# Idle matmuls on TensorE in every eighth expert, another order in the PLE stage, and the last gate tile computed in two parts

## The reference

```
for i in range(2):
    x = x + mixer_i(rmsnorm(x) * norm_mix[i])      # 0: dilated attention, 1: latent attention (MLA)
    x = x + moe(rmsnorm(x) * norm_moe[i])          # 32 experts, top 1 group of 4, top 2 experts in it
    gate = sigmoid((rmsnorm(x) * norm_ple[i]) @ ple_w_gate[i])     # (256,1024) @ (1024,1024)
    x = x + (p[i] @ ple_w[i]) * gate
return rmsnorm(x) * norm_final
```

## Time and profile before

| what | value |
|---|---|
| median of 3 runs | 1388.43 us (1388.11, 1388.43, 1392.02) |
| the profiled execution | 1391.07 us, its span 1389.2 us |
| PE busy | 1057.8 us, 76% of the span |
| DVE, ACT busy | 457.7 us, 292.8 us |
| DMA | 469.97 MB, 338 GB/s over the span |
| mean granted clock of PE | 0.901 |

### The profile page before, as it was taken

One profiled execution on the slowest core, in us unless ns is written; L12 is line 12 of the kernel. 1 busy time (PEld: TensorE's weight loads), 2 busy tenths in 40 slices (PEclk: granted clock), 3 DMA queues, 4 the chain that ended last, 5 costly groups with the idle time before them and its releaser, 6 DMA issues.

```text
span 1389.2 us, 30964 instructions
## 1 busy us (share of the span) xinstructions
PE 1057.8 (76%) x13756; PEld 821.9 (59%) x13756; DVE 457.7 (33%) x1017; ACT 292.8 (21%) x555; POOL 9.2 (1%) x19
## 2 busy tenths in 40 slices
PE   6999999988666667667667989976666666666667
PEld 6999999865545445444445645555444444444446
DVE  6545555552212111111114666521121211121127
ACT  5433444220100000000004444310000000000016
POOL 1000000000000000000000000000000000000000
PEclk9999999999988877988898999998888888898899
DMA  9996540699999999999999740499999999999980
GB/s 272 310 239 175 159 119 0 267 367 426 425 426 426 427 426 426 426 426 426 426 427 393 276 177 1 148 425 427 426 426 426 427 426 426 426 426 427 426 365 35
DMA packets 113483, 469.97 MB, mean 338 GB/s; under 512 B 4656, under 2 KB 78512, under 8 KB 88528
## 3 DMA queue, kind: packets, MB, share of 16 engines
q1 hardware_dynamic: 112672, 465.78, 83.7%
q0 software_dynamic: 688, 2.28, 0.4%
HBM read 467.00 MB, written 1.05 MB: 337 GB/s over the span
## 4 chain that ended last, share of the span: by engine, by line
DMA 49%; PE 44%; DVE 3%; issue 2%; ACT 1%; DVEq 0%; SPq 0%; ACTq 0%
DMA ring<-moe_w_down 33%; DMA ring<-moe_w_up 8%; PE ps L1608 6%; DMA ring<-ple_w_gate 5%; PE ps L1379 5%; PE ps L1380 5%; PE ps L1381 5%; PE ps L1623 4%; PE ps L1695 3%; DMA ring<-moe_w_gate 3%; PE ps L1493 2%; PE ps L1653 2%; PE ps L1514 1%; PE ps L1443 1%; PE ps L1419 1%
## 5 line engine op out<-in xcount | busy, mean ns | idle before, releaser
L1608 PE MATMUL ps<-ring,scr 128*32 128x128 f32 x8192 | 291.2, 302 | 161.3 <-DMA ring<-moe_w_up 103.8
L1608 PEld LDWEIGHTS ps<-ring,scr 128*32 128x32 f32 x8192 | 252.6, 122 | 202.2 <-DMA ring<-moe_w_up 115.0
L1623 PE MATMUL ps<-ring,scr 128*32 128x256 f32 x2048 | 170.0, 485 | 114.8 <-DMA ring<-moe_w_down 100.6
L1623 PEld LDWEIGHTS ps<-ring,scr 128*32 128x32 f32 x2048 | 83.5, 134 | 183.3 <-issue 103.7
L1131 DVE TENSOR_TENSOR scr<-scr,ps 128x128 f32<-128x128 f32 x64 | 23.8, 372 | 445.9 <-PE ps L1608 445.9
L716 ACT COPY scr<-ps 32x256 f32<-32x256 f32 x128 | 46.8, 366 | 557.2 <-PE ps L1623 556.5
L1144 DVE COPY scr<-ps 32x256 f32<-32x256 f32 x128 | 53.3, 416 | 239.0 <-PE ps L1623 238.2
L1379 PE MATMUL ps<-hT_hi,w_qk_hi 128*128 128x256 f32 x368 | 104.4, 284 | 0.0
L1381 PE MATMUL ps<-hT_hi,w_qk_lo 128*128 128x256 f32 x368 | 103.7, 282 | 0.0
L1380 PE MATMUL ps<-hT_lo,w_qk_hi 128*128 128x256 f32 x368 | 103.6, 281 | 0.0
L1653 PE MATMUL ps<-scr 128*128 128x512 f32 x128 | 63.1, 639 | 15.5 <-DVE scr L1144 15.5
(11 more groups left out here) (239 smaller groups left out, 1182.3 us busy)
## 6 DMA issues: line engine op xcount, KB each, us to landing
ring<-moe_w_gate SPq DMA_DIRECT2D x64, 2048.0 KB, 36.0
ring<-moe_w_up SPq DMA_DIRECT2D x64, 2048.0 KB, 36.4
ring<-moe_w_down SPq DMA_DIRECT2D x64, 2048.0 KB, 36.3
ring<-dsa_w_in SPq DMA_DIRECT2D x72, 512.0 KB, 6.8
ring<-ple_w_gate SPq DMA_DIRECT2D x4, 2048.0 KB, 37.3
ring<-dsa_w_out SPq DMA_DIRECT2D x2, 2048.0 KB, 13.6
ring<-mla_w_out SPq DMA_DIRECT2D x2, 2048.0 KB, 24.5
x_sb<-ple_w SPq DMA_DIRECT2D x2, 1024.0 KB, 6.2
```

The lines of the kernel that those rows point to most:

```text
L1608: mm = pe.matmul(bank(b)[CW * q:CW * q + CW, 0:P], xT[:, k, :], tile(t + j, KD, FF)[:, k, P * q:P * q + P], start=(k == 0), stop=(k == KD ...
L1623: mm = pe.matmul(bank(6)[CW * q:CW * q + CW, 0:T], e_hT[:, CW * j:CW * j + CW], tile(t + 2, FF // P, D)[:, j, T * q:T * q + T], start=(j = ...
```

## The change

Three things are changed together.

1. **Idle matmuls.** In the eighth expert of each pass PE runs two matmuls of `ident` by 512 columns of `hs` into bank 6 after the `gate` matmuls and two after the `up` matmuls (`stay_busy`). Nobody reads them.
2. **The start of the PLE stage.** `EARLY` is 2. ACT copies chunk 0 of x first, makes 2 high pieces, copies chunk 1, casts the turned x and then makes the other 6. DVE splits nothing before its copies. PE no longer waits for all 8 high pieces: it takes each k as it comes, and runs low by high two steps behind high by high.
3. **The tail.** The last (chunk 1, half 1) is computed in two parts of `PART` = 256 columns, in banks 3 and 2 (`gate_part`); in layer 0 the turn of chunk 0 stands between the parts. ACT takes the squares of both first halves, and DVE that of chunk 1's second half. Sigmoid, product and sum of the last tile run in two parts. In the final norm DVE multiplies the first half by the gain (`final_gain`) and ACT by the reciprocal (`final`), DVE does the second half, and SP stores four pieces of 256 KB.

The core of the diff:

```diff
-EARLY = 5
+EARLY = 2
+GATES = 5
+PART = 256
 ACT, ple(l):
-                act.wait_ge(S("scattered"), (NGRP + 1) * l + NGRP)
+                take_x(0)
                 high_gate(0, range(EARLY))
-                take_x(0)
-                high_gate(0, range(EARLY, KD))
                 take_x(1)
...
+                high_gate(0, range(EARLY, KD))
                 high_gate(1, range(KD))
...
+                i = 3 * l + 3
+                for c in range(TC):
+                    wait_x(act, i, c, 0)
+                    act.activation(junk_pd[c], x_sb[:, c, 0:512], ACT.Square, accum_out=ss[:, c, 0:1]).then_inc(S("sq_d"), 1)
                 table(ACT.Sqrt)
...
+                table(ACT.Sigmoid)
+                for h in range(2):
+                    act.wait_ge(S("pg_ready"), GATES * l + 4 + h)
+                    act.activation(p_sig[:, 1, 512 + PART * h:512 + PART * h + PART], bank(3 - h)[:, 0:PART], ACT.Sigmoid,
+                                   scale=rstd[:, 1:2]).then_inc(S("sig_ready"), 1)
                 table(ACT.Sqrt)
-                norm_chunk(3 * l + 3, 1)
+                if l == 1:
+                    final(0)
...
 DVE, ple(l):
-                low_gate(0, range(EARLY - 1))
                 for c in range(TC):
                     take_x(c)
...
-                low_gate(0, range(EARLY - 1, KD))
+                low_gate(0, range(KD))
...
                 for c in range(TC):
                     add(c, 0)
-                    square(i, c)
-                for c in range(TC):
-                    add(c, 1)
-                    roots(i, c, c + 1)
-                    finish(c)
+                add(0, 1)
+                if l == 1:
+                    final_gain(0)
+                roots(i, 0, 1)
+                finish(0)
+                if l == 1:
+                    final_gain(1)
+                link(add_part(l, 0))
+                add_part(l, 1).then_inc(S("x_added"), 1)
+                wait_x(dve, i, 1, 1)
+                last = x_sb[:, 1, 512:D]
+                dve.tensor_tensor_reduce(out=junk_pa[1], in0=last, in1=last, scale=1.0, scalar=0.0,
+                                         op0=ALU.mult, op1=ALU.add, accum_out=ss[:, 1, 1:2]).then_inc(S("sq_a"), 1)
+                roots(i, 1, 2)
+                finish(1)
...
 PE, experts(l):
+                def stay_busy():
+                    for _ in range(2):
+                        pe.matmul(bank(6), ident, hs[:, 0, 0:4, :], start=True, stop=True)
...
                             mm.then_inc(S("gate_ready" if j == 0 else "up_ready"), 1)
+                            if i == BODY - 1:
+                                stay_busy()
...
 PE, ple(l):
+                def gate_part(h):
+                    if h == 1:
+                        pe.wait_ge(S("sig_ready"), GATES * l + 2)
+                    cols = slice(PART * h, PART * h + PART)
+                    for x_k, w in ((hT_hi, g_hi), (hT_lo, g_hi), (hT_hi, g_lo[l])):
+                        for k in range(KD):
...
+                for k in range(EARLY, KD):
+                    for c in range(TC):
+                        high_by_high(c, k)
+                    low_by_high(k - EARLY)
...
+                gate_part(0)
+                if l == 0:
+                    turn_rows(3, 0)
+                gate_part(1)
```

More of the change, by code:

```diff
@@ L122, in used @@
             return ("gate_ready", "up_ready", "down_ready")[n % 3], NE * l + n // 3 + 1
-        return "pg_ready", 2 * TC * l + TC * (t - Tiles.PLE[l] + 1)
+        return "pg_ready", GATES * l + (GATES if t > Tiles.PLE[l] else TC)
 C_ID, C_LOW, C_CAUSAL = 0, 128, 256
@@ L731, in experts, with final @@
                     act.wait_ge(S(f"o_down{l}"), NE + 1)
+            def final(c):
+                act.wait_ge(S("x_gained"), c + 1)
+                act.wait_ge(S("rstd_ready"), 6 * TC + c + 1)
+                act.activation(x_sb[:, c, 0:512], p_w[:, c, 0:512], ACT.Copy, scale=rstd[:, c:c + 1]
+                               ).then_inc(S("final_a"), 1)
             def ple(l):
@@ L770, in ple @@
                     sigmoid(c, n)
+                i = 3 * l + 3
+                for c in range(TC):
+                    wait_x(act, i, c, 0)
+                    act.activation(junk_pd[c], x_sb[:, c, 0:512], ACT.Square, accum_out=ss[:, c, 0:1]).then_inc(S("sq_d"), 1)
                 table(ACT.Sqrt)
-                norm_chunk(3 * l + 3, 0)
-                sigmoid(1, 1)
-                table(ACT.Sqrt)
-                norm_chunk(3 * l + 3, 1)
+                norm_chunk(i, 0)
+                table(ACT.Sigmoid)
[3 more added lines that the diff above has]
+                                   scale=rstd[:, 1:2]).then_inc(S("sig_ready"), 1)
+                table(ACT.Sqrt)
+                if l == 1:
+                    final(0)
+                act.wait_ge(S("var_ready"), TC * i + 2)
+                act.activation(root[:, 1:2], root[:, 1:2], ACT.Sqrt, scale=1.0 / D).then_inc(S("root_ready"), 1)
+                if l == 0:
+                    act.wait_ge(S("rstd_ready"), TC * i + 2)
+                    scale(i, 1)
+                else:
+                    final(1)
             table(ACT.Sqrt)
@@ new lines, in gate_part @@
+                def gate_part(h):
[4 more added lines that the diff above has]
+                        for k in range(KD):
+                            x_1 = x_k[:, 1, k, :] if x_k is hT_hi else x_k[:, k, P:2 * P]
+                            mm = pe.matmul(bank(3 - h)[:, 0:PART], x_1, w[1][:, k, cols], start=(x_k is hT_hi and w is g_hi and k == 0),
+                                           stop=(w is not g_hi and k == KD - 1))
+                    mm.then_inc(S("pg_ready"), 1)
@@ new lines, in high_by_high, with low_by_high, high_by_low @@
+                def high_by_high(c, k):
+                    if c == 0:
+                        pe.wait_ge(S("g_high"), 2 * KD * l + k + 1)
+                    pe.wait_ge(S("hT_high"), high + 2 * c + k // 4 + 1)
+                    gate(c, 0, k, hT_hi, g_hi[0], first=(k == 0))
+                def low_by_high(k):
+                    for c in range(TC):
+                        pe.wait_ge(S("hT_low"), low + 2 * c + k // 4 + 1)
+                        gate(c, 0, k, hT_lo, g_hi[0])
+                def high_by_low(c, n):
+                    for k in range(KD):
+                        if c == 0:
+                            pe.wait_ge(S("g_low"), 2 * KD * l + KD * n + k + 1)
+                        mm = gate(c, n, k, hT_hi, g_lo[l][n], last=(k == KD - 1))
+                    mm.then_inc(S("pg_ready"), 1)
@@ new lines, in ple @@
+                for c in range(TC):
+                    for k in range(EARLY):
+                        high_by_high(c, k)
+                for k in range(EARLY, KD):
+                    for c in range(TC):
+                        high_by_high(c, k)
+                    low_by_high(k - EARLY)
+                for k in range(KD - EARLY, KD):
+                    low_by_high(k)
+                for c in range(TC):
+                    high_by_low(c, 0)
+                pe.wait_ge(S("g_high"), 2 * KD * l + 2 * KD)
@@ L1728, in _ @@
+                for k in range(KD):
+                    gate(0, 1, k, hT_hi, g_hi[1], first=(k == 0))
+                for k in range(KD):
+                    gate(0, 1, k, hT_lo, g_hi[1])
+                high_by_low(0, 1)
+                gate_part(0)
+                if l == 0:
+                    turn_rows(3, 0)
+                gate_part(1)
             experts(0)
```

57 lines of the change are left out of this document (21 added, 36 removed).

## The result

The changed kernel took **1391.40 us**, the median of 20 runs (1389.15 to 1396.01), against 1388.14 us for the kernel before in the same session (20 runs, 1385.06 to 1393.21). The ratio is 1.0022 with a 95% interval of 1.0012 to 1.0032: slower by about 3.1 us, less than the 0.3% that the prediction took as its bound, and 2.3 us above the forecast of 1389.1. It is inside the outer range (1386.2 to 1392.4) and 0.8 us above the forecast's own (1387.6 to 1390.6). The profiled execution took 1392.20 us, its span 1390.4.

A forecast was written before the change was run, and what follows sets the result against it. The prediction took the weight stream to bound the experts, so only both layers' PLE stages could gain: 1391.07 - 0.2 (layer 0) - 1.8 (layer 1) = 1389.1 us, own range 1387.6 to 1390.6, outer 1386.2 to 1392.4.

The forecast's parts named there:

- outer range: Whole kernel: 1386.2 to 1392.4 us, chance 0.86, taking in the forecast and nearly all of its neighbouring rivals.
- the turns of chunk 0 follow the scatter without a gap at 752.1: Layer 0, PLE start: earlier copies let PE's turns start at 752.1 instead of 754.90 us.
- The wait for `hs`: Layer 0, before the turn for MLA: PE stands 4.15 us with nothing to do.
- the low clock behind it: Layer 0, from the turn for MLA: the wait very likely lowers PE's clock, costing 1.4 us.
- the likeliest case: Whole kernel: the forecast of 1389.1 us, own range 1387.6 to 1390.6, chance 0.56.
- rival (a): Layer 0: the wait before the turn leaves the clock high; 1387.6 us, chance 0.16.
- (b): Layer 0: clock stays low through all of `gate_part(1)`; 1390.9 us by the profile, 1392.4 at most, chance 0.17.
- an earlier start helps layer 0: Layer 0, PLE stage: (0,1) ready 5.05 us earlier, mostly given back; stage ends 0.2 us earlier.
- forecast 1.8 us better: Layer 1, the tail to the last store: gain 1.8 us, bounds 0.5 and 2.5.
- put at zero: Idle matmuls, both layers: no gain, as the stream covers them and expert 31's `down` tile lands late anyway.
- rival (c): Expert 31, both layers: idle matmuls run at half clock, `down` 2.4 us late in each; 1393.8 us, chance 0.06.
- the same number from both sides: Whole kernel: counting from the low runs, with clock high at stage starts, gives 1388.8 to 1390.2 us.

The follow-up runs named there:

- e1: The changed kernel without its idle matmuls; 1394.02 us, ratio 1.0041 to the kernel before.
- e3: The changed kernel with the turn of x chunk 0 for MLA moved behind both parts of the last gate tile; 1390.30 us, ratio 1.0015 to the kernel before.
- e4: The changed kernel with layer 0's MLA weight transfers issued only after the first cast of the turned x; 1393.06 us, ratio 1.0039 to the kernel before.
- e5: The changed kernel with the old end of the PLE stage in layer 0, the new one in layer 1; 1393.20 us, ratio 1.0027 to the kernel before.
- e7: The changed kernel with 48 never-executed matmuls added to the body of PE's overflow branch in layer 0; 1392.52 us, ratio 1.0020 to the kernel before.
- e2: The kernel before with the idle matmuls alone added; 1390.93 us, ratio 1.0017 to the kernel before.
- e8: The kernel before with the changed end of the PLE stage in layer 1 alone, no idle matmuls; 1388.50 us, ratio 0.9997 to the kernel before.
- e6: The changed kernel without PE's overflow branch (flag read, If and body) in layer 0; 1386.78 us, ratio 0.9986 to the kernel before.
- e9: The changed kernel with the body of PE's overflow branch in layer 0 cut to one matmul; 1386.81 us, ratio 0.9986 to the kernel before.
- e11: The kernel before without PE's overflow branch in both layers; 1390.82 us, ratio 1.0017 to the kernel before.
- e12: The changed kernel with the old end in layer 0 and without PE's overflow branch in both layers; 1386.93 us, ratio 0.9988 to the kernel before.
- e10: The changed kernel without PE's overflow branch in both layers and without idle matmuls; 1387.75 us, ratio 1.0001 to the kernel before.

## Why the prediction held, and where it was wrong

**The step that failed** is "the turns of chunk 0 follow the scatter without a gap at 752.1", for layer 0. The trace of before had the clue, and I read past it: the 14 turns behind the first two had 0.23 us of "issue" ahead of them and started 3.74 us behind the scatter's end at 752.08:

```profile
755.82 3.25 PE L1373 MATMUL ps<-cst,x_sb 128*128 128x128 f32 x14 [0.23 <-issue]
```

In the changed kernel it is 3.77, in e1, e3, e4, e5 and e7 3.59 to 3.78, in e2 4.17: one delay, that the copies' 2.83 us covered all but the end of. In e8 a slower scatter covered more of it. I named the wait that the change removes and didn't ask what was late next. e6 and e9 show what it hangs on; with it gone the turns start 0.17 us before the scatter's modelled end, as forecast.

**What followed in layer 0 was sized right.** Against the scatter's end: (0,1) was forecast at 19.7 us, and e6 has its sigmoid at 19.3; the turn for MLA 26.6 against 25.45; MLA 31.9 against 30.64. The changed kernel, with the hole, has 23.2, 29.4 and 34.66. The wait for `hs` (forecast 4.15, measured 3.35 in both), the low clock behind it, and the end of the low clock inside `gate_part(1)` came as the likeliest case had them, so neither rival (a) nor (b) came. The price of that low clock can be read off e7, where the wait was 3.21 us and the clock stayed high: from the turn to MLA 3.81 us, against 5.29 in the changed kernel. That is 1.48, and I had taken 1.4. Of the 1.26 us by which e6 is earlier than the forecast 0.9 is DVE: I left the second `low_gate` where it was, ending 19.3 us behind the scatter's end, a figure that I had carried over from layer 1 (layer 0's own was 19.83), and it ends at 18.43, since its four early pieces and the gap no longer delay the splits of x.

**The larger claim, that an earlier start helps layer 0, is weak.** e11 (old start) reaches MLA 30.44 us behind the scatter, e12 and e6 (new start) 30.41 and 30.64. PE comes to the turn for MLA earlier (27.56 us behind the scatter in e11, 25.45 in e6) and gives it back from there to MLA (2.88 us in e11, 5.19 in e6: more gates behind the turn, and these at the low clock). Against the profile of before the stage is 1.4 us shorter in e6, but it is 1.6 shorter in e11 too, which has the old start. The cleanest pair is e10 and e11, both without the branch and without idle matmuls, so that only the start and the ends differ. Layer 0 is the same (30.89 and 30.44 us), layer 1 from `down` to the last store 3.65 us shorter (37.94 and 41.59), and the medians 3.1 us apart, with intervals that overlap. With idle matmuls and the old end in layer 0 (e12 against e11) the ratios are 0.29% apart and the intervals don't overlap. What the change is worth lies in layer 1.

**Layer 1** was forecast 1.8 us better and is 2.78. From the start of the last `low_gate` (1366.41, now 1369.83) to the last store's issue it is 20.15 against 18.29: 1.86, the term as forecast. Within it the part up to the last sigmoid's end won 1.88 (15.54 to 13.66; forecast 1.6), and the part behind it nothing (4.61 and 4.63; forecast 0.2). The missing 0.92 is again DVE's `low_gate`, 13.97 us behind the scatter before and 13.05 now. e8 adds that this needs the new start.

**The idle matmuls** were put at zero, and on the profile of before that is right: `up` at half clock was hidden by the tile of `down`. But I took that one profile for all. In the nine profiles with idle matmuls (changed, e2 to e7, e9, e12) all 18 `up` and scatter stretches had the high clock. In the five without (before, e1, e8, e10, e11), of ten stretches six had the low clock in `up` alone, hidden; one in `up` and `down` (e1), two in `up`'s successors, the scatters (e8), and one never. That they hold the clock is shown. What it is worth is less plain: only e1's stretch reached the end. Of the 3.0 us that its tail is longer (40.99 against 37.95) the low clock of `down` made 1.7, and the hole ahead of the turns the rest; the others lay under a tile or under the old start. e1 against the changed kernel (2.6 us) and e10 against e6 (1.0 us) speak for them, e2 against the kernel before (2.7 us slower with them) against them, each with intervals that overlap or nearly reach 1. My rival (c), that they would run at half clock themselves, came in none.

**The sum.** The hole less DVE's gain makes 2.8 us more in layer 0 than forecast (34.66 against 31.9), layer 1 gives 1.0 more: 1389.1 + 2.8 - 1.0 = 1390.9. That the measured 1391.4 is near proves little. The sum starts from the profiled execution of before, 1391.07, which lay 2.9 us above the median of its kernel. From that median, 1388.14, the same two stages (+2.65, -2.78) give 1388.0, so 3.4 us of the difference in medians stand in no stage that I forecast; where they lie is open. My argument from the low runs, "the same number from both sides", isn't borne out. Better matched is e6 against the changed kernel: the stage 4.0 us shorter, the runs 0.36%, 5 us. Rival (b)'s 1390.9 "by the profile" is also a slip: 1391.07 + 2.0 - 1.8 is 1391.3. The terms that I named were near, but for the delay that I had not seen; that the time lay inside my bounds with it is luck.

The drain of about 1380 ns that the Trainium skill ("ScalarE: Activation LUTs", "What ACT_TABLE_LOAD costs") puts on top of each table load, and that I weighed in the prediction, isn't in this trace. The load at 1378.65 takes 1.28 us and the next square begins at 1380.05, 1.40 us after its start, with a small activation between, as the row of before had it.

## What stays open

Shown is that layer 0's delay goes away when the long body isn't there to be jumped over. That a long jump alone makes it isn't shown: the same jump in layer 1 costs nothing in the changed kernel, e3, e4, e6 and e9. That PE has to fetch its instructions anew there is argued, not shown: the page counts 114 packets of 16 KB on the instruction queue, without naming an engine. Why the hole stands ahead of the first turn in some kernels, two turns on in others (before, e1, e8), and in layer 1 only in e1 (1.19 us), e5 (2.82 us) and e7 (1.78 us), isn't settled. Nor is the difference of 3 us between the medians of the changed kernel and the one before. Not tried was a kernel that keeps its full branch and places it so that nothing waits: e6, e9 and e12 leave the overflow work of layer 0 out, so they show what is to be had, 0.12 to 0.14% or some 2 us under the kernel before, and aren't yet a kernel to use.

## What to carry to other kernels

When a wait goes, look for the small "issue" gap next to it: it may be the uncovered tip of a delay as long as the wait. Count it from events of the engine itself, not from the releaser that the profile names, and look when that releaser ended. A long body that is seldom entered may cost something where it stands ahead of the stretch that sets the end; try the kernel without it. And compare stages between fixed events, over several kernels, before a difference of 3 us is believed.

## What I had not expected of the hardware

- Behind a jump over a body of 56 matmuls and their waits PE's turns in layer 0 went on 3.6 to 3.8 us after the scatter's end in seven kernels (4.17 in e2, 1.45 in e8); behind one over a single matmul there was no gap (e9). The same jump in layer 1 cost nothing in five kernels.
- 48 matmuls that never run made a hole of 1.78 us some 600 us later (e7), and an edit in layer 0 one of 2.82 us (e5): the same instructions in another place take another time.
- The hole left the clock at 2.4 GHz in the changed kernel (turns in 1.94 us), and lowered it in e3, e4, e5 and e7 (3.48 to 3.65 us for the same 16).
